# Block attention of the second block, computed for two heads at a time instead of one, inside the recurrence over chunks

## What is computed

```python
logits = jnp.einsum('bhqd,bhqnkd->bhqnk', qq, kg).astype(jnp.float32) * scale
...
logits = jnp.where(mask, logits, -jnp.inf)
p = jax.nn.softmax(logits.reshape(B, H, MOBA_QCHUNK, nsel * MOBA_BLOCK), axis=-1)
...
return jnp.einsum('bhqnk,bhqnkd->bhqd', p, vg)
```

```python
sa = jnp.einsum('bhij,bhj->bhi', state, -kk_t)
state = (state * w_t[:, :, None, :]
         + sa[..., :, None] * (kk_t * a_t)[:, :, None, :]
         + v_t[..., :, None] * k_t[:, :, None, :])
return state, jnp.einsum('bhij,bhj->bhi', state, r_t)
```

## Time and profile before

| | |
|---|---|
| median of 3 runs | 3247.49 us (3246.6 to 3247.62) |
| the profiled execution's own time | 3245.86 us |
| its span | 3244.0 us |
| TensorE busy | 3153.3 us (97%) |
| VectorE, ScalarE busy | 1371.9 us (42%), 599.2 us (18%) |
| DMA | 585.39 MB, mean 180 GB/s |

### The profile page before, as it was taken

The page is one execution under the profiler, slowest core; times in us unless marked ns, Lnnn a source line. Parts: engine busy times, 40 slices in busy tenths (PEclk is TensorE's granted clock), DMA queues, the critical chain, the costliest instruction groups (busy, mean ns, idle before and its releaser), DMA issues.

```text
span 3244.0 us, 35828 instructions
## 1 busy us (share of the span) xinstructions
PE 3153.3 (97%) x14634; PEld 1959.6 (60%) x14634; DVE 1371.9 (42%) x2564; ACT 599.2 (18%) x1240; POOL 1.4 (0%) x6
## 2 busy tenths in 40 slices
PE   8999999999999999999899999999999999999998
PEld 5855554334333333358696588888546444588887
DVE  4256530110110111155735354466363994264655
ACT  2143220110010010021444311002231002120001
POOL 0000000000000000000000000000000000000000
PEclk9999999999999999999998999999999999999999
DMA  6122369999999999941000222222202112122221
GB/s 268 63 78 82 108 253 404 428 428 429 429 428 429 428 429 428 429 176 64 27 1 24 81 78 91 92 85 100 78 27 75 71 71 74 74 86 97 78 78 52
DMA packets 43100, 585.39 MB, mean 180 GB/s; under 512 B 4768, under 2 KB 6816, under 8 KB 7648
## 3 DMA queue, kind: packets, MB, share of 16 engines
q1 hardware_dynamic: 42752, 582.45, 44.1%
q0 software_dynamic: 224, 1.18, 0.1%
HBM read 581.51 MB, written 2.10 MB: 180 GB/s over the span
## 4 chain that ended last, share of the span: by engine, by line
PE 86%; DMA 9%; DVE 3%; ACT 1%; issue 1%; SPq 0%; DVEq 0%; ACTq 0%
PE PS L482 20%; PE PS L294 12%; PE PS L1670 11%; PE PS L686 10%; DMA ring<-in_weights 5%; PE PS L1648 4%; DMA A<-in_weights 4%; PE PS L1246 3%; PE PS L374 3%; PE PS L1593 2%; PE PS L348 2%; PE PS L1634 1%; PE PS L1575 1%; PE PS L2198 1%; PE PS L1038 1%; PE PS L1203 1%
## 5 line engine op out<-in xcount | busy, mean ns | idle before, releaser
L482 PE MATMUL PS<-A 128*128 128x256 f32 x1336 | 298.4, 379 | 0.0
L1670 PE MATMUL PS<-ring,A 128*64 128x512 f32 x1248 | 284.8, 598 | 1.5 <-DMA ring<-in_weights 1.1
L482 PEld LDWEIGHTS PS<-A 128*128 128x128 f32 x1336 | 253.6, 190 | 35.6 <-issue 0.8
L294 PE MATMUL PS<-H,ring 128*128 128x512 f32 x544 | 234.4, 592 | 0.7 <-issue 0.7
L1752 DVE TENSOR_TENSOR A<-A,PS 64x512 f32<-64x512 f32 x64 | 44.1, 690 | 434.7 <-ACT A L1699 434.7
L482 PE MATMUL PS<-H,ring 128*128 128x256 f32 x784 | 185.3, 379 | 0.8 <-ACT A L1785 0.8
L1670 PEld LDWEIGHTS PS<-ring,A 128*64 128x64 f32 x1248 | 82.7, 136 | 168.0 <-issue 160.8
L294 PEld LDWEIGHTS PS<-H,ring 128*128 128x128 f32 x544 | 103.3, 190 | 130.3 <-issue 130.2
L1670 PE MATMUL PS<-A 128*64 128x512 f32 x784 | 178.4, 598 | 1.9 <-ACT A L1710 0.4
L686 PE MATMUL PS<-A 128*128 128x256 f32 x800 | 178.7, 379 | 0.0
L1648 PE MATMUL PS<-A 128*64 128x512 f32 x768 | 174.1, 598 | 3.3 <-DMA A<-in_weights 3.1
(11 more groups left out here) (534 smaller groups left out, 4071.5 us busy)
## 6 DMA issues: line engine op xcount, KB each, us to landing
ring<-in_weights SPq DMA_DIRECT2D x176, 2048.0 KB, 14.1
A<-in_weights SPq DMA_DIRECT2D x96, 2048.0 KB, 24.3
X<-in_x SPq DMA_DIRECT2D x1, 2048.0 KB, 12.9
H<-in_weights SPq DMA_DIRECT2D x1, 2048.0 KB, 13.4
A<-in_weights SPq DMA_DIRECT2D x2, 768.0 KB, 23.7
vec<-in_vec SPq DMA_DIRECT2D x1, 1047.0 KB, 11.1
A<-in_ctx SPq DMA_DIRECT2D x1, 1024.0 KB, 19.1
out_y<-X SPq DMA_DIRECT2D x2, 512.0 KB, 2.9
```

The costliest lines, as they stand in the source:

```text
L294: mm = nc.tensor.matmul(bank[:, 0:out_width], weight_tile(name, n), moving(k), start=k == 0, stop=k == k_tiles - 1)
L482: mm = nc.tensor.matmul(pair_bank(name, p, n), w[:, k, :], x[:, k, :], start=k == 0 and not more, stop=k == 3, skip_group_check=more)
L1670: mm = nc.tensor.matmul(PS[CAP * up:CAP * (up + 1), c % 2, :], XS[:, k, CAP * b:CAP * (b + 1)], expert_tile(slot, 8 * (k % 4) + 4 * up), s ...
```

## The change

The units are taken two heads at a time. Step `s` of twelve now holds the same 128 queries (`qt = s % 4`) of the even and the odd head of pair `s // 4`: `two_heads(u)` gives the head and `qt` of unit `u`. The two scores of a step are issued one behind the other: their contractions lie in the upper and the lower 64 partitions, and they write banks 3 and 4. The outputs of both heads of a pair are issued together, key tile by key tile in turns; they write partitions 0 to 63 and 64 to 127 of bank 7. The order within a step is turned round: the step first waits for both exponentials of its own units (`att_exp`) and issues the scores of the next step, then, at the start of a pair, the outputs of the pair before, then the transposes of its two units. ScalarE copies both transposed units first and then takes both exponentials of the next step; VectorE's order stays two maxima, two normalisations. No instruction of VectorE or ScalarE is added or dropped. The third block's attention keeps its order (`head_by_head`).

```diff
+        def moba_scores(pe, s):
+
+            for u in (2 * s, 2 * s + 1):
+                h, qt = two_heads(u)
+                n = (qt + 1) * P
+                nc.tensor.matmul(PS[:, 3 + u % 2, 0:n], A[half64(h), MQ + h // 2, qt * P:n], MKEYS[half64(h), h // 2, 0:n],
+                                 start=True, stop=True).then_inc(S["att_scores"], 1)
+
+        def moba_outputs(pe, p):
+
+            pe.wait_ge(S["att_turned"], 2 * TT * (p + 1))
+            if p:
+                pe.wait_ge(S["att_heads"], 2 * p)
             for kt in range(TT):
-                mm = nc.tensor.matmul(o[:, kt * P:], MVTOK[:, kt, 64 * h:64 * h + 64], MPT[h % 2][:, kt, kt * P:],
-                                      start=kt == 0, stop=True, skip_group_check=kt > 0)
-            mm.then_inc(S["att_out"], 1)
-
-        def moba_steps(pe, u0):
-
-            for u in (u0, u0 + 1):
+                for h in (2 * p, 2 * p + 1):
+                    mm = nc.tensor.matmul(PS[half64(h), 7, kt * P:], MVTOK[:, kt, 64 * h:64 * h + 64],
+                                          MPT[h % 2][:, kt, kt * P:], start=kt == 0, stop=True, skip_group_check=kt > 0)
+                    if kt == TT - 1:
+                        mm.then_inc(S["att_out"], 1)
+
+        def moba_step(pe, s):
+
+            if s + 1 < UNITS2 // 2:
+                pe.wait_ge(S["att_exp"], 2 * s + 2)
+                moba_scores(pe, s + 1)
+            if s and s % TT == 0:
+                moba_outputs(pe, s // TT - 1)
+            for u in (2 * s, 2 * s + 1):
                 pe.wait_ge(S["att_probs"], u + 1)
                 if u >= 2:
                     pe.wait_ge(S["att_turned"], u - 1)
-                for kt in range(u % TT + 1):
-                    mm = nc.tensor.transpose(PS[:, 5 + u % 2, kt * P:(kt + 1) * P], MPROB[u % TT][:, kt * P:(kt + 1) * P], ident)
+                for kt in range(two_heads(u)[1] + 1):
+                    mm = nc.tensor.transpose(PS[:, 5 + u % 2, kt * P:(kt + 1) * P], MPROB[u % 4][:, kt * P:(kt + 1) * P], ident)
                 mm.then_inc(S["att_turn"], 1)
-                if u + 2 < UNITS2:
-                    moba_score(pe, u + 2)
-                if u and u % TT == 0:
-                    moba_output(pe, u // TT - 1)
...
+        def moba_step_act(act, s):
+            for u in (2 * s, 2 * s + 1):
+                att_turned(act, 0, u, two_heads, 5 + u % 2, MPT)
+            if s + 1 < UNITS2 // 2:
+                moba_exps(act, s + 1)
+            if s and s % TT == 0:
+                moba_leave(act, s // TT - 1)
```

More of the change, by code:

```diff
@@ L2189, in three_blocks @@
         AMX, ANM, ASUM, AREC = (small[:, 256 + 32 * j:288 + 32 * j] for j in range(4))
+        head_by_head = lambda u: (u // TT, u % TT)
+        two_heads = lambda u: (2 * (u // (2 * TT)) + u % 2, u % (2 * TT) // 2)
         def attention_tensor(pe, h0, heads, parts, v_tok, rows):
@@ L2221, in attention_tensor, with att_exp @@
                 mm.then_inc(S["att_out"], 1)
-        def att_exp(act, h0, u, scale, bank, prob):
-            n = (u % TT + 1) * P
+        def att_exp(act, h0, u, place, scale, bank, prob):
+            n = (place(u)[1] + 1) * P
             act.wait_ge(S["att_max"], TT * h0 + u + 1)
@@ L2227, in att_exp, with att_turned @@
                                  accum_out=ASUM[:, u:u + 1]).then_inc(S["att_exp"], 1)
-        def att_turned(act, h0, u, bank, pt):
-            h, qt = u // TT, u % TT
+        def att_turned(act, h0, u, place, bank, pt):
+            h, qt = place(u)
             act.wait_ge(S["att_turn"], TT * h0 + u + 1)
             if h >= 2 and qt == 0:
-                act.wait_ge(S["att_out"], h0 + h - 1)
+                act.wait_ge(S["att_out"], h0 + (h - 1 if place is head_by_head else h - h % 2))
             nc.scalar.activation(pt[h % 2][:, 0:qt + 1, qt * P:(qt + 1) * P], as_tiles(PS[:, bank, 0:(qt + 1) * P]),
@@ L2239, in att_leave, with att_max @@
             nc.scalar.activation(dest, PS[rows, bank, :], ACT.Copy).then_inc(S["att_heads"], 1)
-        def att_max(dve, h0, u, scale, bank):
-            qt = u % TT
+        def att_max(dve, h0, u, place, scale, bank):
+            qt = place(u)[1]
             dve.wait_ge(S["att_scores"], TT * h0 + u + 1)
@@ L2264, in attention_act @@
                     att_leave(act, h0, h, 6 + h % 2, dest(h), rows(h))
-            att_turned(act, h0, units - 1, 4 + (units - 1) % 2, PT_)
+            att_turned(act, h0, units - 1, head_by_head, 4 + (units - 1) % 2, PT_)
             att_leave(act, h0, heads - 1, 6 + (heads - 1) % 2, dest(heads - 1), rows(heads - 1))
@@ L2269, in attention_dve @@
             for u in range(TT * heads):
-                att_max(dve, h0, u, scale, u % TT)
+                att_max(dve, h0, u, head_by_head, scale, u % TT)
                 if u:
-                    att_normalise(dve, h0, u - 1, PROB[:, (u - 1) % TT, :])
-            att_normalise(dve, h0, TT * heads - 1, PROB[:, TT - 1, :])
+                    att_normalise(dve, h0, u - 1, head_by_head, PROB[:, (u - 1) % TT, :])
+            att_normalise(dve, h0, TT * heads - 1, head_by_head, PROB[:, TT - 1, :])
         half64 = lambda h: slice(64 * (h % 2), 64 * (h % 2) + 64)
@@ L2312, in moba_steps, with moba_exps, moba_leave, moba_step_dve @@
                     pe.wait_ge(S["att_turned"], u - 1)
-                for kt in range(u % TT + 1):
-                    mm = nc.tensor.transpose(PS[:, 5 + u % 2, kt * P:(kt + 1) * P], MPROB[u % TT][:, kt * P:(kt + 1) * P], ident)
+                for kt in range(two_heads(u)[1] + 1):
+                    mm = nc.tensor.transpose(PS[:, 5 + u % 2, kt * P:(kt + 1) * P], MPROB[u % 4][:, kt * P:(kt + 1) * P], ident)
                 mm.then_inc(S["att_turn"], 1)
-                if u + 2 < UNITS2:
-                    moba_score(pe, u + 2)
-                if u and u % TT == 0:
-                    moba_output(pe, u // TT - 1)
[L2321 to L2337, removed]
+        def moba_exps(act, s):
+            for u in (2 * s, 2 * s + 1):
+                att_exp(act, 0, u, two_heads, 64 ** -0.5, 3 + u % 2, MPROB[u % 4])
+        def moba_leave(act, p):
+            for h in (2 * p, 2 * p + 1):
+                att_leave(act, 0, h, 7, A[half64(h), MQ + p, :], half64(h))
+        def moba_step_act(act, s):
+            for u in (2 * s, 2 * s + 1):
+                att_turned(act, 0, u, two_heads, 5 + u % 2, MPT)
[3 more added lines that the diff above has]
+                moba_leave(act, s // TT - 1)
+        def moba_step_dve(dve, s):
+            if s < UNITS2 // 2:
+                for u in (2 * s, 2 * s + 1):
+                    att_max(dve, 0, u, two_heads, 64 ** -0.5, 3 + u % 2)
+                for u in (2 * s, 2 * s + 1):
+                    att_normalise(dve, 0, u, two_heads, MPROB[u % 4])
         def low_rank_tensor(p):
@@ L2658, in rwkv_tensor @@
                 mm.then_inc(S["y_chunk"], 1)
-                moba_steps(pe, 6 * c + 4)
-            moba_output(pe, HEADS2 - 1)
+                moba_step(pe, 3 * c + 2)
+            moba_outputs(pe, PAIRS2 - 1)
             banks = [open_bank("wout2", f) for f in range(3)]
@@ L2763, in rwkv_act @@
                                                  ).then_inc(S["nx_out"], 1)
-            for u in range(2):
-                att_exp(act, 0, u, 64 ** -0.5, 3 + u, MPROB[u])
+            moba_exps(act, 0)
             for c in range(4):
@@ L2771, in rwkv_act @@
                 v.then_inc(S["w_out"], 1)
-                moba_steps_act(act, 6 * c)
-                moba_steps_act(act, 6 * c + 2)
+                moba_step_act(act, 3 * c)
+                moba_step_act(act, 3 * c + 1)
                 act.wait_ge(S["y_chunk"], c + 1)
```

37 lines of the change are left out of this document (13 added, 24 removed).

## The result

The changed kernel takes 3229.59 us (median of 4 runs, 3229.06 to 3230.48); the kernel before, run beside it, 3247.55. The ratio is 0.9941, with a 95% interval of 0.9929 to 0.9953: 15 to 23 us faster, 18 by the medians. The forecast was 14.1 us. The direction came out, and the pairing gave what was forecast; the size was too small, as the clock's share of the gain was put at nothing. By the ratio, 0.9941 × 3247.49 = 3228.3 us, the time lies just under the range. That it lies outside at all is no firm result: one of the four runs before took 3253.06 us, the others 3246.6 to 3247.62, and by the medians (0.9945) or by the second set (0.9949) it is 3229.6 or 3230.9, inside.

A forecast was written before the change was run, and what follows sets the result against it. The prediction took TensorE, busy 97% of the span, to bound the kernel. Outputs −6.4, scores −6.4, shapes −4.5, waits +3.2 and clock 0 summed to −14.1 us, so 3247.49 becomes 3233.4 us, range 3228.5 to 3241.

The forecast's parts named there:

- Outputs: Attention outputs in the recurrence stage: two heads alternating between column halves take what one took, −6.4 us.
- Scores and shapes: Recurrence stage: scores paired by row halves, −6.4 us; fewer changes between transposes, scores and outputs, −4.5 us (bounds 3.5 and 5).
- The open bound: Scores: halving assumed from the recurrence's short quadrant passes, as no long row-paired matmuls were traced; other end no overlap, 0.
- The third rival: Scores: row halves don't run together with long moving operands, 6.4 us lost, total −7.7 us; chance 0.08.
- Waits: TensorE waiting for both exponentials of a step before issuing the next scores: +3.2 us, bounds 1 and 6.
- The layout's absolute sums: TensorE's waits over all twelve steps laid out: 5.5 us in the new order, 2.3 in the old.
- Clock: Recurrence stage: 17 us at 1.2 GHz cost 8.5 us before and would last as long again, term 0.
- the earlier return: Chunk 0: paired halves fill the array, so full clock may return some 3 us earlier, worth 1.7 us.
- the new fall: Clock falls again or returns later in the stage: 7 to 20 us more at half, −10.6 to −4.1; chance 0.16.
- its own signs of being wrong: Scores x4 in 1.9 us, clock under 1.00 in chunks 1 to 3, or stage gaining 14 us without the span.
- The slower case: Clock stays at half after chunk 0 for the rest of the stage: some 95 us, +20; chance 0.04.
- a later stage gives the gain back: Fourth rival: neither pair overlaps, or a later stage gives the gain back, −1 to −2 us; chance 0.06.

The follow-up runs named there:

- the second set: The changed kernel run once more, unedited, against the kernel before: 3230.89 us, ratio 0.9949, stage 58.37 us.
- e1: The changed kernel with a pair's outputs issued head by head, so column halves don't alternate: ratio 0.9963 to the kernel before, stage 61.31 us.
- e3: The changed kernel with score, transposes, score, transposes by turns within a step, outputs still paired: ratio 0.9967 to the kernel before, stage 64.74 us.
- e5: The kernel before with 16 identity transposes filling TensorE's wait ahead of the first scores: ratio 0.9979 to the kernel before, stage 68.64 us.
- e4: The changed kernel with 16 identity transposes filling TensorE's wait ahead of the first scores: ratio 0.995 to the kernel before, stage 53.76 us.
- e8: The changed kernel with 8 identity transposes ahead of the step behind u in chunks 2 and 3: ratio 0.9941 to the kernel before, stage 56.65 us.
- e2: The changed kernel, each pair's second score waiting until the first is complete: ratio 0.9983 to the kernel before, stage 67.76 us.
- e6: The changed kernel with the first halves of delta and y issued ahead of the step behind u: ratio 0.9936 to the kernel before, stage 56.58 us.
- e9: e7 with ScalarE taking both exponentials of the next step ahead of this step's copies: 3222.77 us, ratio 0.9926 to the kernel before, stage 53.19 us.
- e10: e7 with ScalarE's copies and exponentials by turns: ratio 0.994 to the kernel before, stage 52.94 us.
- e7: The changed kernel with the edits of e6 and e4 together: 3224.08 us, ratio 0.9926 to the kernel before, stage 52.94 us.

## Why the forecast missed its size

**Outputs, right.** Forecast −6.4 and 0.5 of shape; measured 4.6 to 2.3 a pair, −6.9. The reason given, alternation, carries 4.7 of it (e1); the rest comes from the overlap of two heads that are issued one behind the other.

**Scores and shapes, right in sum, in part by luck.** Forecast 10.6 for both (6.4, and 12 × 0.35); e3 against the change gives 9.1. Another 1.8, which makes up for the difference, lies between e3 and the kernel before (75.30 − 64.74 = 10.6, less 1.7 of clock, 0.1 of idle time and 6.9 of outputs) and was in no term: the turned order puts the transposes directly ahead of w and u, which have their shape. The w row is 1.45 long, where it was 1.55, and three transposes ahead of u take 0.38 (1740.39 to 1740.77 in e3) where ahead of a score they take 0.47 (1738.86 to 1739.33). Eight such places make 1.5 of the 1.8; no run tries this alone. The work's sum, 6.9 + 9.1 + 1.8 = 17.8, stands against 17.3 forecast and 18.3 by the busy times at full clock. The open bound, whether long matmuls in two row halves run together, was taken from the row of the recurrence's quadrants, and it held: 1.06 us for two scores as for one, 2.19 when they are kept apart. The third rival (row halves don't run together) is out.

**Waits, right.** Forecast +3.2, measured +3.45 at full clock (e5, e4) and +2.6 in the profiles. The layout's absolute sums, 5.5 and 2.3, fit the stages at full clock (5.17 and 1.72); with chunk 0 at half clock they were 3.71 and 1.08. The two long ones were laid out as 1.4 and 1.0 behind the u piece in chunks 2 and 3 and measured 1.14 and 0.98; the 0.7 behind u in chunk 1 was 0.15. e8 has the first of the long ones filled, and with it the fall of the clock behind it is gone.

**Clock, the step that failed:** "If they last as long again, they cost as much, and the term is 0." They did not last as long: 10.24 us at half in chunk 0, then 3.41 in chunk 2, together 13.65 against 17.07. By the filled kernels that is −2.1 us: 4.57 us of clock in the change against 6.66 before. The 8.5 us at which the prediction put the clock's cost before was too high as well (e5). Full clock was back 11.5 us after the first scores, not 18. The forecast had named the earlier return (1.7) and the new fall as things that could happen and had put both outside the sum; both happened, and the clock of 0.89 in chunk 2 is one of its own signs of being wrong. That the return is early because paired scores keep more of the array at work is supported: with the scores kept apart the half clock in chunk 0 lasted 17.07 us (before, e2) or 13.65 (e3), and 10.24 in all five profiles with paired scores and the wait ahead of them (the change twice, e1, e6, e8). It isn't shown alone, as keeping the scores apart also moves what TensorE does in time.

**The sum.** The terms −6.4 − 6.4 − 4.5 + 3.2 = −14.1 stand against −14.9 at full clock, and −2.1 of clock make −17.0; the profiled executions differ by 3245.86 − 3229.06 = 16.8, the medians by 18.0. The last 1.2 us between these lie in the spread of the runs. Of the 14.88 us at full clock the forecast had all but 0.8; the larger part of what it missed is the clock's 2.1. The range's lower end, −19, already held an early clock together with its best waits. Only the first of the two came, as the waits were 3.45 and not 1, and by the ratio the time was still 0.2 us below, less than the runs of one kernel differ. With the clock's 2.1 in the sum, the forecast would have been −16.2.

**The other rivals.** The slower case needed 28 us more at half clock; there were 3.4 less. That a later stage gives the gain back did not occur in the change, but did in e4. The clock fell behind 1.95 us of idle time ahead of the stage, and with that filled it did not (e4, e5); in both profiles of the change it fell behind 1.14 us, and with that filled it did not (e8). The Trainium skill's page "TensorE: Matmul & The Clock Gate", section "Why this matters for your kernels", warns only of gaps longer than any here; the traces don't agree with it as a safe bound, though the same 1.14 us cost nothing in e1 and e4.

## What to carry to other kernels

In this kernel matmuls that use half the rows or half the columns of TensorE cost as much as whole ones until two of different halves are issued next to each other; then two cost what one did (1.06 us for scores, 2.31 for a head's outputs), and grouping them also saves 0.15 to 0.2 us for each change of shape. Read what is worth pairing from a pair that the kernel already has. When work on TensorE shrinks, put its clock in the sum from the start: measure the stage once with the idle time ahead of it filled, so that work and clock can be priced apart.

## What the runs showed of the hardware

*One wait, two outcomes.* The third block's attention ends with three idle times of TensorE. In the change:

```profile
2433.36 0.55 PE L2213 MATMUL PS<-con,A 128*128 128x128 f32 x3 [1.36 <-DVE A L2256]
2434.85 0.66 PE L2213 MATMUL PS<-con,A 128*128 128x128 f32 x4 [0.95 <-DVE A L2256]
2436.20 2.42 PE L2222 MATMUL PS<-A 128*128 128x512 f32 x8 [0.69 <-ACT A L2237]
2439.31 11.00 PE L294 MATMUL PS<-A,ring 128*128 128x512 f32 x25 [0.69 <-ACT A L2242]
```

and in e4, whose program is the same there:

```profile
2427.77 0.55 PE L2213 MATMUL PS<-con,A 128*128 128x128 f32 x3 [1.36 <-DVE A L2256]
2429.27 1.04 PE L2213 MATMUL PS<-con,A 128*128 128x128 f32 x4 [0.95 <-DVE A L2256]
2430.99 4.63 PE L2222 MATMUL PS<-A 128*128 128x512 f32 x8 [0.69 <-ACT A L2237]
2436.31 14.00 PE L294 MATMUL PS<-A,ring 128*128 128x512 f32 x32 [0.69 <-ACT A L2242]
```

The same waits (1.36, 0.95, 0.69 us), but in e4 the clock fell at 2429.4 for 6.8 us: the outputs took 4.63 us instead of 2.42, and with 3.4 us more at half near 2818 what stands behind the stage took 1470.9 us instead of 1466.6. It was 1466.6 (within 0.1) in both profiles of the change, in the kernel before, e1, e3 and e5; 1470.9 in e2 and e4; and 1464.9 in e6, e9 and e10, where a fall of 3.4 us near 1830 to 1850 was missing. In e7 (1469.0) and e8 (1468.0) that fall was missing and those near 2430 and 2820 were there. So after an edit in one stage waits that were harmless can cost the clock, or the other way about, 4 us up or 2 down. What decides it isn't shown: the edits shift all that follows in time, but e2, whose stage is 9 us longer than the change's, and e4, whose stage is 5 us shorter, fell alike. An edit of some us is therefore read by its stage and not by the whole time: e4's stage is 4.6 us shorter than the change's, and its whole time is no less.

*TensorE doesn't start passes strictly in the order of the program.* With the outputs head by head (e1), the first pass of the second head starts at 1725.27 beside the fifth of the first head's eight, in the other column half, and not behind the eighth. Together with the one coming to the shape saved, that is 0.72 of the 2.3 us that a pair of heads gains.
